# Two transformer blocks on one core: norms fed tile by tile, squares beside the additions, a recut opening, one semaphore clear

## The reference, cut to what matters

```python
def rms_norm(x, g):
    y = x * lax.rsqrt(jnp.mean(x * x, axis=-1, keepdims=True) + 1e-6)
    return y * g
def modulate(h, shift, scale):
    return h * (1.0 + scale) + shift

# block 1; sh*, sc*, ga* (and csh*, csc* of the context) = split(silu(c) @ w_mod + b_mod, 6)
px = modulate(rms_norm(x, norm_mix), sh1, sc1) @ w_in        # 2048 -> 5568
pc = modulate(rms_norm(ctx, norm_mix), csh1, csc1) @ w_in
yx = concat([rwkv_mix(...), short_conv_mix(px), fourier_mix(px)]) @ w_out
x = x + ga1 * yx                                             # stage "out1"
x = x + ga2 * ffn(modulate(rms_norm(x, norm_ffn), sh2, sc2)) # "norm2", "ffn1"; d_ff = 5632
x = rms_norm(x, norm_final)
# block 2
p_lat, p_ctx = modulate(rms_norm(x, g)) @ w_in_2, modulate(rms_norm(ctx_2, g)) @ w_in_2  # "in2"
x = x + gt_m * (concat([hgrn2(...), window_attention(...)]) @ w_out_2)  # "out2" is its end
x = x + gt_f * swiglu(modulate(rms_norm(x, norm_ffn_g_2)))              # "norm5", "ffn2"
```

## Time and profile before

| | us |
|---|---|
| median of 3 runs (lowest, highest) | 3861.1 (3860.64, 3867.76) |
| profiled execution | 3860.53 |
| its span, first to last instruction | 3858.8 |
| PE busy / DVE busy / ACT busy | 3641.5 (94%) / 2228.0 (58%) / 537.3 (14%) |
| busy PE, 1242 to 1272 us (`norm2`) | 10.83 of 30 |
| mean granted clock of TensorE | 0.972 |

### The profile page before, as it was taken

The page is one execution under the profiler, slowest core; times in us unless marked ns, Lnnn a source line. Parts: engine busy times, 40 slices in busy tenths (PEclk is TensorE's granted clock), DMA queues, the critical chain, the costliest instruction groups (busy, mean ns, idle before and its releaser), DMA issues. The chain is left out here.

```text
span 3858.8 us, 66595 instructions
## 1 busy us (share of the span) xinstructions
PE 3641.5 (94%) x29287; PEld 3094.6 (80%) x29287; DVE 2228.0 (58%) x4273; ACT 537.3 (14%) x991; POOL 82.8 (2%) x86
## 2 busy tenths in 40 slices
PE   6999999989989899999999899999989899999999
PEld 4466666667767899999999467667767899999999
DVE  4265555555334788889866545555552666654644
ACT  2222122222100100000000312322221100000000
POOL 0000000000000000000000000000000000000000
PEclk8989999999999999999999999999999999999999
DMA  9622333333348587787667254534413566664553
GB/s 342 209 73 76 86 96 93 88 86 105 87 158 275 181 259 240 243 262 230 191 219 241 93 176 149 162 115 152 153 66 129 161 202 203 202 196 156 167 164 126
DMA packets 680354, 637.94 MB, mean 165 GB/s; under 512 B 42093, under 2 KB 670338, under 8 KB 678658
## 3 DMA queue, kind: packets, MB, share of 16 engines
q1 hardware_dynamic: 569120, 558.96, 45.6%
q10 hardware_dynamic: 110946, 74.73, 6.7%
HBM read 627.36 MB, written 6.29 MB: 164 GB/s over the span
## 5 line engine op out<-in xcount | busy, mean ns | idle before, releaser
L1828 PE MATMUL bank<-extra,work 128*128 128x128 f32 x4224 | 478.9, 275 | 0.0
L1828 PEld LDWEIGHTS bank<-extra,work 128*128 128x128 f32 x4224 | 475.2, 192 | 0.0
L623 DVE SCALAR_TENSOR_TENSOR work<-weight_ring,silu_c,work 128x256 f32<-128x256 f32 x1050 | 421.0, 476 | 0.0
L1828 PE MATMUL bank<-work,weight_ring 128*128 128x128 f32 x2816 | 328.0, 278 | 30.5 <-PEq L717 30.5
L1828 PEld LDWEIGHTS bank<-work,weight_ring 128*128 128x128 f32 x2816 | 322.0, 194 | 31.2 <-issue 31.2
L1972 DVE TENSOR_TENSOR work<-weight_ring 128x2048 f32<-128x2048 f32 (+1 forms) x76 | 129.3, 1701 | 304.4 <-DMA weight_ring<-in_w_gate_up 169.2
L965 PE MATMUL bank<-work,x_channels 128*128 128x256 f32 (+1 forms) x736 | 247.7, 476 | 4.4 <-ACT work L1335 3.9
L1884 PE MATMUL bank<-work,weight_ring 128*128 128x128 f32 x2112 | 247.2, 275 | 0.0
L1884 PEld LDWEIGHTS bank<-work,weight_ring 128*128 128x128 f32 x2112 | 241.7, 192 | 3.3 <-issue 3.3
L2352 PE MATMUL bank<-work,weight_ring 128*128 128x512 f32 x448 | 205.5, 604 | 2.1 <-PEq L2141 2.1
L965 PEld LDWEIGHTS bank<-work,x_channels 128*128 128x128 f32 x736 | 137.2, 199 | 73.7 <-issue 52.3
(11 more groups left out here) (400 smaller groups left out, 5294.0 us busy)
## 6 DMA issues: line engine op xcount, KB each, us to landing
weight_ring<-in_w_mod SPq DMA_DIRECT2D x80, 2048.0 KB, 9.6
weight_ring<-in_w_gate_up SPq DMA_DIRECT2D x44, 2048.0 KB, 9.5
weight_ring<-in_w_in SPq DMA_DIRECT2D x26, 2048.0 KB, 9.9
weight_ring<-in_w_down SPq DMA_DIRECT2D x32, 1536.0 KB, 6.9
weight_ring<-in_w_gate SPq DMA_DIRECT2D x22, 2048.0 KB, 8.2
weight_ring<-in_w_up SPq DMA_DIRECT2D x22, 2048.0 KB, 11.8
weight_ring<-in_w_down SPq DMA_DIRECT2D x32, 1280.0 KB, 6.1
weight_ring<-in_w_out SPq DMA_DIRECT2D x16, 2048.0 KB, 9.2
```

The costliest lines, as they stand in the source:

```text
L623: ins = v_.scalar_tensor_tensor(a, w[:, k, :], c, a, ALU.mult, ALU.add)
L1828: last = mm(out[:, m * P:(m + 1) * P], left[p][:, k, m * P:(m + 1) * P], right[p][:, k, :], start=k == 0, stop=k == 7)
```

## The change

- `normalise` and its two stages are gone. A helper `RowSquares` lets ACT square each tile of `xT` right after DVE's addition (in `out1` and `out2`), and TensorE adds the squares up in bank 4 with one matmul per tile, two slots' tiles late in `out1` and two tiles late in `out2`. `ffn` then begins with root (ACT) and reciprocal (DVE), and each of the 16 tiles is scaled on DVE (gain and reciprocal root in one instruction) and shifted on ACT; the first unit's matmuls wait for one tile at a time.
- `out1` uses four banks in place of two.
- `in2` takes the block i first, its products on the context before those on x, and prepares all context tiles before those of x; order now i, f0, f1, q, g.
- In `opening`, ACT copies four of the eight context groups out of the banks; the context is squared in two halves and summed over its tiles by TensorE (16 matmuls) rather than by DVE's reduction; the reduction for x comes after the evacuations; the first products of `w_in` come after two `mod_sum`s rather than five, and each pair's products are split around a `mod_sum`.
- In `rwkv` the wait for tanh and sigmoid moves behind the first filling work and the key norms.
- In `ffn1` the two loads of the second context go from ACT's queue to SP's, ahead of the loads for `in2`.
- Semaphores are cleared after `rwkv` alone.

```diff
+class RowSquares:
+    def __init__(self, nc, st, name):
+        self.nc, self.st = nc, st
+        self.buf = st.carve(8192, 2, T)
+        self.s_squared, self.s_summed = st.sem(f"{name}_squared"), st.sem(f"{name}_sumsq")
+    def square(self, act, m):
+        if m >= 2:
+            act.wait_ge(self.s_summed, m - 1)
+        self.nc.scalar.activation(self.buf[:, m % 2, :], self.st.xT[:, m, :], ACT.Square).then_inc(self.s_squared, 1)
+    def add(self, pe, m):
+        pe.wait_ge(self.s_squared, m + 1)
+        self.nc.tensor.matmul(self.st.psum[4][:, 0:T], self.st.c("ones"), self.buf[:, m % 2, :], start=m == 0, stop=m == KT - 1
+                              ).then_inc(self.s_summed, 1)
@@ out_projection, tensor
-                        last = nc.tensor.matmul(st.psum[half][:, 0:T], w[:, k, half * P:(half + 1) * P], rhs(k),
+                        last = nc.tensor.matmul(st.psum[(2 * s + half) % 4][:, 0:T], w[:, k, half * P:(half + 1) * P], rhs(k),
                                                 start=k == 0, stop=k == KT - 1)
+                if s:
+                    rows.add(pe, 2 * s - 2)
+                    rows.add(pe, 2 * s - 1)
@@ ffn: sync, tensor (first unit), scalar, vector
+            if bridge:
+                stream_weights(sp, st, n)
+                for t in range(2):
+                    sp.wait_ge(S["product"], 4 * (U + 4 * (D - 1) + 1 + t))
+                    sp.dma_start(ctok[t], st.dram["ctx_2"][t * P:(t + 1) * P, :]).then_inc(S[f"ctx_in{t}"], 16)
+                            if u == 0 and m == 0 and j < 2:
+                                pe.wait_ge(S["h_ready"], 8 * j + k + 1)
+            nc.scalar.activation(rstd, st.psum[4][:, 0:T], ACT.Sqrt, bias=st.eps[:, 0:1], scale=1.0 / DM).then_inc(S["root"], 1)
+            for k in range(KT):
+                act.wait_ge(S["scaled"], k + 1)
+                nc.scalar.activation(h[:, k, :], h[:, k, :], ACT.Identity, bias=shift[:, k:k + 1]).then_inc(S["h_ready"], 1)
+            vl(v_.reciprocal(rstd, rstd))
+            for k in range(KT):
+                v_.scalar_tensor_tensor(h[:, k, :], xT[:, k, :], gain[:, k:k + 1], rstd, ALU.mult, ALU.mult).then_inc(S["scaled"], 1)
+            dve.wait_ge(S["h_ready"], KT)
@@ in2
-IN2_DENSE = ((0, "f0"), (2, "f1"), (4, "q"), (6, "i"), (8, "g"))
+IN2_DENSE = ((0, "i"), (2, "f0"), (4, "f1"), (6, "q"), (8, "g"))
+                        if j in (0, 2):
+                            pe.wait_ge(s_h, j // 2 * KT + k + 1)
@@ opening, tensor
-            for s in range(MOD_FIRST):
-                mod_sum(s)
-                if s:
-                    mod_column(s - 1)
-                if s < 2:
-                    sums_of_squares(s)
-                elif s % 2 == 0 and s >= 4:
-                    project(s // 2 - 2)
-            mod_column(MOD_FIRST - 1)
-            project(KT // 2 - 2)
+            mod_sum(0)
+            sums_of_squares(1)
+            sums_of_squares(0)
+            mod_column(0)
+            mod_sum(1)
+            mod_column(1)
+            for pair in range(KT // 2 - 1):
+                s = 2 * pair + 2
+                if pair:
+                    mod_sum(s)
+                    project(pair, (0,))
+                else:
+                    project(pair, (0,))
+                    mod_sum(s)
+                mod_sum(s + 1)
+                mod_column(s)
+                project(pair, (1,))
+                mod_column(s + 1)
             project(KT // 2 - 1)
@@ rwkv, tensor
-            W("lora_act", 2)
             fill(FILL["first"])
             key_norms(0)
             fill(FILL["first"])
+            W("lora_act", 2)
@@ program
-            if name in ("opening", "rwkv", "ffn1", "hgrn"):
+            if name == "rwkv":
```

More of the change, by code:

```diff
@@ L429, in _ @@
             a_(st.silu_c[:], st.par[:, 0:64], ACT.Silu).then_inc(st.s_silu, 1)
-            act.wait_ge(S["x_evac"], KT)
-            a_(sq[1], hT[:, :, seg[1]], ACT.Square).then_inc(S["squared"], 1)
+            for j, m in enumerate((9, 11, 13, 15)):
+                act.wait_ge(S["x_T"], m + 1)
+                nc.scalar.copy(hT[:, 2 * m - 16:2 * m - 14, 0:L], st.psum[2 + m % 4][:].rearrange("p (a b) -> p a b", a=2)).then_inc(S["c_evac"], 1)
+            for half in range(2):
+                act.wait_ge(S["x_evac"], 10 + 2 * half)
+                act.wait_ge(S["c_evac"], 2 + 2 * half)
+                a_(sq[1][:, 8 * half:8 * half + 8, :], hT[:, 8 * half:8 * half + 8, seg[1]], ACT.Square).then_inc(S["squared"], 1)
             def add_shift(pair):
@@ L496, in mod_column, with project @@
                 last.then_inc(S["mod_columns"], 1)
-            def project(pair):
+            def project(pair, parts=(0, 1)):
                 pe.wait_ge(S[f"w_in{pair // 2}"], 64)
                 if pair == 0:
-                    pe.wait_ge(S["x_evac"], KT)
+                    pe.wait_ge(S["x_evac"], KT - 4)
+                    pe.wait_ge(S["c_evac"], 4)
                     pe.wait_ge(S["root"], 2)
                 last_pair = pair == KT // 2 - 1
-                for i in range(2 if not last_pair else 1):
+                for i in parts if not last_pair else (0,):
                     pe.wait_ge(S["h_ready"], 2 * (2 * pair + i + 1 + last_pair))
@@ L585, in _ @@
                 dve.wait_ge(S["mod_kept"], s + 1)
-                if s < 2:
-                    dve.wait_ge(S["root"], s + 1)
-                    vl(v_.reciprocal(rstd[:, s, :], rstd[:, s, :]))
-                if s == 1:
+                if s == 0:
+                    for v in range(2):
+                        dve.wait_ge(S["root"], v + 1)
+                        vl(v_.reciprocal(rstd[:, v, :], rstd[:, v, :]))
                     scale(0)
@@ L1674, in credit @@
     def credit(self, dve):
[L1675 removed]
+        dve.sem_inc(self.s_free, 4)
     def bank_free(self, pe, u, half, i=0, per=0):
@@ L1716, in _ @@
                         side.columns(pe, at[s])
+                if s:
+                    rows.add(pe, 2 * s - 2)
+                    rows.add(pe, 2 * s - 1)
             if mods:
                 side.flush(pe)
+            rows.add(pe, KT - 2)
+            rows.add(pe, KT - 1)
+        @block.scalar
+        def _(act):
+            for m in range(KT):
+                act.wait_ge(res.s_free, 4 + m + 1)
+                rows.square(act, m)
         @block.vector
@@ L1732, in _, with ffn @@
                 gain_columns(nc, st, 0, "norm_ffn", 64, 0, 2)
-def ffn(nc, st, name, which, mods):
+def ffn(nc, st, name, which, mods, gain, shift):
     first, _ = SPANS[name]
-    S = {x: st.sem(f"{name}_{x}") for x in ("tokens_ready", "product", "post", "gated", "silu", "G", "mod_step",
+    S = {x: st.sem(f"{name}_{x}") for x in ("root", "scaled", "h_ready", "tokens_ready", "product", "post", "gated", "silu", "G", "mod_step",
                                             "mod_columns", "mod_kept", "down_ready", "p1", "squared", "sumsq", "ctx_in0",
@@ L2212, in _ @@
             dve.wait_ge(s_root, 1)
+            vl(v_.reciprocal(rc, rc))
+            for x, k in turn[:4]:
+                scale(x, k)
+            dve.wait_ge(s_root, 2)
             vl(v_.reciprocal(ra, ra))
@@ L2215, in _ @@
             v_.tensor_tensor(q, q, ra, ALU.mult).then_inc(s_var, 1)
-            dve.wait_ge(s_root, 2)
-            vl(v_.reciprocal(rc, rc))
-            for x, k in turn[:4]:
+            for x, k in turn[4:KT]:
                 scale(x, k)
@@ L2222, in _ @@
             vl(v_.tensor_tensor(q, ra, rb, ALU.mult))
-            for x, k in turn[4:]:
+            for x, k in turn[KT:]:
                 scale(x, k)
@@ L2822, in out_projection2 @@
     gate = st.mod[1][:, 0, 32:48]
+    rows = RowSquares(nc, st, "out2")
     with nc.Block() as block:
@@ L2838, in _ @@
                     pe.sem_inc(st.s_slot_used, 1)
+                if m >= 2:
+                    rows.add(pe, m - 2)
+            rows.add(pe, KT - 2)
+            rows.add(pe, KT - 1)
+        @block.scalar
+        def _(act):
+            for m in range(KT):
+                act.wait_ge(s_added, m + 1)
+                rows.square(act, m)
         @block.vector
```

104 lines of the change are left out of this document (39 added, 65 removed).

## The result

The changed kernel takes 3800.3 us (median of 4 runs, 3797.2 to 3801.4) against 3862.0 before: ratio 0.9836, 95% interval 0.9819 to 0.9853. In the profiled executions the spans differ by 60.1 us (3858.75 and 3798.64).

The account below looks back on a forecast made before the run. TensorE was taken to bound the feed-forward, so starting it earlier is gained in full if weights keep up. Terms 23.3 + 13.7 + 4.0 + 2.3 + 1.2 + 2.0 = 46.5 us, from 3860.5: 3814; range 3804 to 3826.

Parts of the forecast that it names:

- norm2: Border from `out1` to the first feed-forward: third product starts at 1256.7, not 1280.52; 23.8 us gained, less 0.5 for weights.
- out1: First output projection: 6.0 us of added column sums replace waits, step 15.15 us, no gain or loss; up to 6 if waits stay.
- norm5: Border from `out2` to the second feed-forward: 14.2 us gained, less 0.5 for weights, with a 1.28 us table load on the path.
- Rival (a): Matmuls fed tile by tile run at a slow clock: 4 us at each feed-forward, 2 at `in2`; 3820 to 3830, chance 0.18.
- Rival (b): More gain: no transfer pause or slow clock in the opening, 5 us, and 2 at `in2` and clears; 3800 to 3808, chance 0.13.
- Rival (c): Feed-forward: loop of weight loads and sums outlasts a unit, TensorE waits in each of 44 units; slower, up to 3884, chance 0.02.
- Rival (d): Feed-forward border is not bound by the norm and weights come late anyway: gain 0, chance 0.01.
- in2: Start of `in2`: first context tile needs only one root and one reciprocal, first matmul about 2150; gain 4.0 us, bounds 1 and 6.
- rwkv's start: Start of `rwkv`: the 7.87 us wait goes, but key norms still need ACT's squares; gain 2.3 us, bounds 0 and 3.
- clears: Stage borders: three semaphore clears go at 0.4 us each, gain 1.2 us, bounds 0 and 2.5.
- opening: Opening: DVE's second reduction leaves the path, first `project` at 51 not 60.47, transfers pause; net gain 2 us, bounds -3 and 6.
- TensorE's 16 matmuls of 0.43 start near 32.5: Opening: sums of the squared context on TensorE start once ACT has squared and end at 39.8; DVE's reduction ended at 47.46.

## Why the prediction was right, and where it was wrong

The total was wrong: 3800.3 lies below the range. Most terms came out by the mechanism that was given for them; one was missing, and one was too small.

- **norm2** (23.8, less 0.5): right. 24.5 from the last column sum to the third product, and the charge of 0.5 for late weights fell away, since `ffn1` from its third product on took 864.30 us (864.22 before). The sum had the sixteenth tile 0.4 us late by its own terms (0.8 and fifteen times 0.40 are 6.8, not 7.2); measured, from the first tile's start to the last one's end, are 7.03.
- **out1** (nothing either way): right, but with the wrong reason, so in part by luck. A step took 15.13 us (1150.43 to 1165.56, forecast 15.15). The four banks are worth 1.8 us of waits; the sums cover the rest.
- **norm5** (14.2, less 0.5): 14.6. The root followed the load of 1.28 us by 0.02 us, so the drain of about 1380 ns that the Trainium skill (ScalarE: Activation LUTs, What ACT_TABLE_LOAD costs) adds is not seen here either. Nor does it stand before a load: the next one in this trace begins 0.02 us behind ACT's copy (2960.51), and of the 86 loads in the trace 39 have less than 0.05 us on both sides.
- **Rival (a)**, slow fed matmuls: the granted clock was 0.53 for the first 5.8 us, while the tiles came (the last at 1238.12), and 1.00 from there on, so most of product 1 was slow and product 4 was not. The premise of half-idle feeding did not hold: TensorE was busy 5.74 of the 5.80 us, and what it lacks in the next 5 us is one wait, the 0.87 for the token sums.

```profile
1232.20:1238.00 5.80, 5.74 (x28) 5.77 (x29) 5.31 (x14) 5.80 (x15) 0.00 (x0) 0.53 1.10 349
1238.00:1243.00 5.00, 4.18 (x38) 3.99 (x36) 4.81 (x5) 0.88 (x3) 0.00 (x0) 1.00 0.46 164
```

- **Rival (b)**: its interval, 3800 to 3808, holds the measured time, but not by its mechanism: the transfers did pause, at 141 GB/s from 50 to 60 us, and the mean granted clock was 0.84 there. Only its 2 us more at `in2` and the clears came.
- **Rival (c)**: did not happen; TensorE waits for no weights in 870 us. The lag that I feared does not build up. Rival (d) fell: the stretch to the third product became 24 us shorter.
- **in2** (4.0): the mechanism was right (first product 4.8 us behind the table load, forecast 4.5), the size too small: 5.6 with its clear by the two main traces, 6.6 by the runs with and without it, and 6.9 by the means of all profiles with either order (132.0 and 125.1 from the end of `ffn1` to `hgrn`, the clear in it in most). I took the products as fed at 0.40 us a tile with pauses charged to them; after 3.75 us and a wait of 0.31 they ran through without another.
- **rwkv's start** (2.3): right to 0.1 in this pair. Over the other profiles the stretch took 10.3 to 11.2 us in the old order and 9.1 to 10.7 in the new, so part of this is luck.
- **clears** (0.4 each): about 0.6 each. From the last instruction of the stage before to the first of the next it took 1.09 us before and 0.51 after at `rwkv`, 0.87 and 0.28 at `in2`. They were not tried by themselves.
- **opening** (2.0 and its clear): right, though one pair of traces says 3.9. The changed kernel's execution has the earliest start of `rwkv` of all, 166.56; the four others with this opening and neither padding nor pause have 167.6 to 169.5 (mean of the five 167.9), the two with the old opening and its clear 170.4 and 169.8. That is 2.2 us on the mean against 2.4 forecast. The first `project` came at 49.5 (forecast 51) and the third `mod_sum` at 56.2 (60); the pause of the transfers came.
- **The failed step**: "TensorE's 16 matmuls of 0.43 start near 32.5": I costed these added sums as 7 us beside other work and nothing else. With them TensorE's program became 66 instructions longer ahead of `rwkv`, which moved every later border of 256 instructions, and that is worth 7.3 us by the profiled executions, 7.8 net by the runs with and without the 66. The term was missing altogether, in a stage that I had down for 2.3 with bounds of 0 and 3 (its start). With it the forecast would have been 3807. The second step that was off is the size of `in2`, 4.0 for 6.6. My own had no sight of it; the waits of `rwkv` have it, under "issue".
- The other 6.3 us by which the profiled difference exceeds the forecast are `in2` with its clear (1.2), the opening (1.5, scatter by the above), the two charges for late weights and `ffn2` (1.4), `hgrn` (1.8) and the norms and attention (0.4). `hgrn` took 549.4 and 550.2 us in the kernel before and the one with the norms only, 547.1 to 549.1 in all others, also in the kernel before with 66 or 106 instructions more; what makes this difference was not tried and stays open.

## What to carry to other kernels

Read the waits of the stages that a change leaves alone too: idle time of TensorE that ends with "issue", in dense runs of small matmuls and always at the same remainder of the instruction count, was here the program arriving late, and added instructions ahead of it shifted the time of that stage by 3 to 13 us, either way. A gain or loss of this size in an untouched stage is no merit of the change: pad the old kernel to the same count and time it before crediting anything, and look in the trace at what the padding itself costs where it stands. Read a term of 2 us off several executions, not off one pair. Where TensorE is the bound and carries filling work, put it ahead of the wait, not behind it, and move none from a place before looking at what it covers there.

## Not expected of the hardware

TensorE's program comes in packets of 16,384 bytes, 256 instructions (231 packets); in blocks of matmuls of 32 rows and 64 columns (192 records in 2.55 us undisturbed) and in the filling beside them it stopped at the borders for 1.3 to 5.7 us, 20 to 40 us in all over `rwkv`. A long stop costs more than itself: within 3 us behind each of the 72 stops of 3.4 us and more the granted clock was at 0.5 (1.2 GHz), behind only 10 of the 57 shorter ones, and 59 records that take 0.8 us at the undisturbed pace took 1.45 us after the stop of 4.16 us that ends at 307.52. Eighty instructions that compute nothing, placed in a wait at the start that was too short for them, made the kernel 16.6 us slower, 9.7 of them in a stage that begins 157 us after them.
